# A decoder step on one core: stacked low-rank columns, values in token rows, and sample scores by head

## The reference, cut to what matters

```python
proj = h @ w_in                      # h = rmsnorm(x)
cb, cc, ch, q, k, v, g, lr = split(proj)      # 512,512,512,256,256,512,512,16 columns
log_a = log_sigmoid(lr @ gate_up + gate_b) / 16
o = gated_linear_attention(q, k, v, log_a)    # 4 heads, 64 keys, 128 values, chunks of 64
y = concat(cb * conv3(cc * ch), rmsnorm(o) * silu(g)) @ w_out
x = x + y
# cross-attention, 4 heads of 256, into 256 memory tokens; each sample has its own keys and values
q = rmsnorm(x) @ w_q
s = einsum('bthd,bmhd->bhtm', q, mk) * 256 ** -0.5
o = einsum('bhtm,bmhd->bthd', softmax(s), mv) @ w_o
x = x + o
# then a mixture of 16 experts and a last rmsnorm
```

## Time and profile before

| | us |
|---|---|
| runs shown | 1178.74, 1178.45, 1171.38 (median 1178.45) |
| the profiled execution | 1174.92 |
| its span, first to last instruction | 1173.0 |
| PE busy in it | 1090.9 (93%) |
| DVE busy | 432.6 (37%) |
| ACT busy | 361.7 (31%) |
| mean granted clock of PE | 0.958 of full speed |

### The profile page before, as it was taken

One profiled execution on the slowest core, in us unless ns is written; L12 is line 12 of the kernel. 1 busy time (PEld: TensorE's weight loads), 2 busy tenths in 40 slices (PEclk: granted clock), 3 DMA queues, 4 the chain that ended last, 5 costly groups with the idle time before them and its releaser, 6 DMA issues.

```text
span 1173.0 us, 14004 instructions
## 1 busy us (share of the span) xinstructions
PE 1090.9 (93%) x5864; PEld 860.4 (73%) x5864; DVE 432.6 (37%) x718; ACT 361.7 (31%) x563; POOL 95.6 (8%) x108
## 2 busy tenths in 40 slices
PE   7999988999999999899999989889998699999995
PEld 6778988888888879688799978658886444444442
DVE  6824421435443542633320047533127321222222
ACT  6725422211111103422122166522112111345453
POOL 1000000000000000000000000000000222344443
PEclk9998989999999998899999999989997699999998
DMA  9561011011101212432121428554225798787831
GB/s 359 165 166 36 19 54 36 19 36 37 37 19 36 78 54 60 156 109 90 56 73 37 179 94 301 218 179 162 108 91 201 287 393 338 309 335 297 329 98 59
DMA packets 85832, 167.48 MB, mean 143 GB/s; under 512 B 19050, under 2 KB 56186, under 8 KB 79364
## 3 DMA queue, kind: packets, MB, share of 16 engines
q1 hardware_dynamic: 72804, 141.14, 34.0%
q0 software_dynamic: 12960, 25.39, 6.1%
HBM read 145.03 MB, written 43.29 MB: 161 GB/s over the span
## 4 chain that ended last, share of the span: by engine, by line
PE 80%; DVE 8%; ACT 5%; DMA 4%; issue 2%; POOL 0%; POOLq 0%; SPq 0%; DVEq 0%; ACTq 0%
PE G L1354 14%; PE G L1280 12%; PE G L1282 11%; PE G L1281 11%; PE G L774 10%; PE G L796 4%; PE G L778 2%; DMA arena<-in_cache_mem_k_dram 2%; PE T L766 2%; PE T L1535 2%; PE T L1371 2%; PE G L1600 1%; PE G L801 1%; PE G L1402 1%; DMA arena<-in_w_o_dram 1%
## 5 line engine op out<-in xcount | busy, mean ns | idle before, releaser
L1280 PE MATMUL G<-act_hi,w_hi 128*128 128x344 f32 (+1 forms) x792 | 264.5, 334 | 13.7 <-DVE arena L1965 4.4
L1281 PE MATMUL G<-act_lo,w_hi 128*128 128x344 f32 (+1 forms) x792 | 257.6, 325 | 0.0
L1282 PE MATMUL G<-act_hi,w_lo 128*128 128x344 f32 (+1 forms) x792 | 257.2, 325 | 0.0
L1280 PEld LDWEIGHTS G<-act_hi,w_hi 128*128 128x128 f32 (+1 forms) x792 | 150.8, 190 | 26.8 <-issue 20.5
L1354 PE MATMUL G<-wt,act_hi 128*128 128x512 f32 x512 | 144.4, 405 | 10.4 <-DVE wt L1951 5.4
L1281 PEld LDWEIGHTS G<-act_lo,w_hi 128*128 128x128 f32 (+1 forms) x792 | 151.0, 191 | 2.6 <-issue 1.2
L1282 PEld LDWEIGHTS G<-act_hi,w_lo 128*128 128x128 f32 (+1 forms) x792 | 150.8, 190 | 1.4
L1354 PEld LDWEIGHTS G<-wt,act_hi 128*128 128x128 f32 x512 | 96.8, 192 | 34.1 <-issue 6.3
L774 PE MATMUL G<-wring,misc 128*128 128x512 f32 x256 | 114.2, 600 | 1.2 <-ACT misc L843 1.2
L666 POOL DMA_INDIRECT misc<-d_h,tidx x20 | 20.5, 1025 | 968.7 <-DVE tidx L987 911.0
L1945 DVE TENSOR_TENSOR w_lo<-arena,w_hi 128x1024 fp32r<-128x1024 f32 (+1 forms) x33 | 39.3, 1192 | 143.5 <-ACT w_hi L1652 143.5
(11 more groups left out here) (340 smaller groups left out, 1385.7 us busy)
## 6 DMA issues: line engine op xcount, KB each, us to landing
wring<-in_w_gate_dram SPq DMA_DIRECT2D x16, 1024.0 KB, 11.2
wring<-in_w_up_dram SPq DMA_DIRECT2D x16, 1024.0 KB, 13.8
wring<-in_w_down_dram SPq DMA_DIRECT2D x16, 1024.0 KB, 16.4
arena<-in_w_in_dram SPq DMA_DIRECT2D x24, 512.0 KB, 3.9
arena<-in_x_prompt_dram SPq DMA_DIRECT2D x16, 512.0 KB, 7.1
d_x<-arena SPq DMA_DIRECT2D x16, 512.0 KB
arena<-in_cache_mem_k_dram SPq DMA_DIRECT2D x8, 1024.0 KB, 7.8
arena<-in_w_k_dram SPq DMA_DIRECT2D x8, 512.0 KB, 6.3
```

Of the source, the lines that this page charges most:

```text
L1280: pe.matmul(out, a_hi, b_hi, start=first, stop=False)
L1281: pe.matmul(out, a_hi, b_lo, start=False, stop=False)
L1282: return pe.matmul(out, a_lo, b_hi, start=False, stop=last)
```

## The change

Three parts are rewritten.

First, `lr`: hi and lo parts of its 16 weight columns are placed side by side as 32 columns (`STACK`). Two matmuls per chunk, with `act_hi` and `act_lo`, take the place of three, and the 32 result rows meet `gate_up` loaded twice, so that their sum is formed in the gate's product.

Second, the values: `w_in`'s value columns are loaded as four blocks of 256 rows by 512 columns, split into the tensor `wt`, and `vtok` computes them in token rows: for nine tiles (eight of 128 tokens, one of 8 samples) 24 matmuls with the tokens as weights and 512 moving columns. Each of the first eight tiles has a PSUM bank of its own (`v_at`), and ACT copies it to `vtm`. No transposes are left. The splits of the four blocks are taken with `k0` and `k1` (the table `MORE`), ahead of `prep`. The attention's steps begin one part later (`steps = [[]]`).

Third, the memory stage: `caches` stands after the first query block. Keys are loaded in eight units, each one head of four samples (`load_keys`, 1 MB in pieces of 1 KB), and queries go to DRAM and back by head (`qh`: store, wait, broadcast of 8 samples x 256). DVE takes a unit's eight multiply-reduces (`ks`) two at a time after query blocks 3, 5 and 7, and the last two after the transposes of tiles 0 and 1. In the tiles' loop the next scores stand right behind the transposes, half of the exponentials stands ahead of them, and four of `w_o`'s splits stand before and after tile 7's transposes (`FINISH`).

```diff
-    for i in range(VB):
-        add("v", i, win, c_v + i * P)
+    for i in range(KB // 2):
+        add("v", i, win, c_v, VB * P)
...
+    MORE = {at[("k", QB - 2)]: [at[("v", i)] for i in range(2)],
+            at[("k", QB - 1)]: [at[("v", i)] for i in range(2, KB // 2)] + [at[("cc", 0)]]}
...
-        if k == "v":
-            order.append(("vT", i))
-
-    steps = []
+    order += [("vtok", t) for t in range(TILES)]
+
+    steps = [[]]
...
     for i in range(KB):
         order.append(("block", at[("mq", i)]))
...
+        h, odd = divmod(i, 2)
+        if i == 0:
+            order.append(("caches", 0))
+        if odd and 1 <= h:
+            order += [("ks", u) for u in (2 * h - 2, 2 * h - 1)]
+        if not odd and h >= 1:
+            order += [("kl", u) for u in (2 * h - 2, 2 * h - 1) if u >= 2] + [("qh", h - 1)]
+    order += [("kl", 2 * MH - 2), ("sc", 0), ("qh", MH - 1), ("kl", 2 * MH - 1), ("max", 0), ("exp", (0, 0, MH)), ("sc", 1), ("rc", 0),
+              ("scl", 0), ("max", 1), ("exp", (1, 0, 2))]
+    FINISH = {NT - 2: [("smax", 0), ("split", at[("o", 0)]), ("split", at[("o", 1)])],
+              NT - 1: [("sprob", 0), ("val", 0), ("split", at[("o", 2)]), ("split", at[("o", 3)]), ("val", 1), ("vload", 0)]}
     for t in range(NT):
         pv = [("pvk", n) for n in range((t - 2) * UP // 2, (t - 1) * UP // 2)] if t >= 2 else []
...
+        order += [("tr", t)] + [("sc", t + 2)] * two + [("exp", (t + 1, 2, MH)), ("rc", t + 1), ("scl", t + 1)] * one + pv[0:1]
+        order += [("max", t + 2), ("exp", (t + 2, 0, 2))] * two + pv[1:2]
+        if t < 2:
+            order.append(("ks", 2 * MH - 2 + t))
...
+            def load_keys(u):
+
+                h, half = divmod(u, 2)
+                sp.dma_start(keys[u % 2], cache_mem_k[0, half * HB:(half + 1) * HB, :, h, :].rearrange("b (m p) d -> p b m d", p=P)).then_inc(
+                    s[f"kc_in{u % 2}"], 16)
...
+                elif what == "kl":
+                    sp.wait_ge(s["q_sc"], i - 1)
+                    load_keys(i)
+                elif what == "qh":
+                    sp.wait_ge(s["q_ev"], i + 1)
+                    if i >= 1:
+                        sp.wait_ge(s["q_io"], 32 * i)
+                    sp.dma_start(d_q[i].rearrange("(b d) -> b d", b=DB), qs[:, i * DH:(i + 1) * DH]).then_inc(s["q_io"], 16)
+                    sp.wait_ge(s["q_io"], 32 * i + 16)
+                    if i >= 2:
+                        sp.wait_ge(s["q_sc"], 2 * (i - 1))
+                    sp.dma_start(qb[i % 2], d_q[i].partition_broadcast(P)).then_inc(s["q_io"], 16)
...
+                        if kind == "lr":
+                            pe.matmul(G[grp[u]][0:STACK, c, 0:cn], w_hi[:, slot, k, 0:STACK], act_hi[:, k, c0:c0 + cn],
+                                      start=(k == 0), stop=False)
+                            ins = pe.matmul(G[grp[u]][0:STACK, c, 0:cn], w_hi[:, slot, k, 0:STACK], act_lo[:, k, c0:c0 + cn],
+                                            start=False, stop=(k == KB - 1))
+                            continue
...
+                    for k in range(KB):
+                        p, half = divmod(k, 2)
+                        if i == 0 and half == 0:
+                            pe.wait_ge(s["split_done"], at[("v", p)] + 1)
+                        ins = mm3(v_at[i][0:r], act_hi[:, k, c0:c0 + r], act_lo[:, k, c0:c0 + r],
+                                  v_half(p, 0)[:, half, :], v_half(p, 1)[:, half, :], k == 0, k == KB - 1)
+                    ins.then_inc(s["v_mm"], 1)
...
+                    dve.wait_ge(s[f"kc_in{i % 2}"], 16 * (h + 1))
+                    dve.wait_ge(s["q_io"], 32 * (h + 1))
```

More of the change, by code:

```diff
@@ L141, in build @@
     order += [("vev", 0), ("memout", 0), ("st", 0)]
-    for n in range(2 * KB, at[("cc", 0)]):
+    for n in range(2 * KB, at[("v", 0)]):
         order.append(("block", n))
@@ L183, in build @@
     order.insert(order.index(("norm", TILES + 1)), ("split", at[("mq", 0)]))
+    PAIRS, UP = NT // 2, KB // 2
+    HB = DB // 2
     for i in range(KB):
         order.append(("block", at[("mq", i)]))
[L187 to L194, removed]
@@ L200, in build @@
[L200 to L202 removed]
+        one, two = t + 1 < NT, t + 2 < NT
+        order += [("tr", t)] + [("sc", t + 2)] * two + [("exp", (t + 1, 2, MH)), ("rc", t + 1), ("scl", t + 1)] * one + pv[0:1]
+        order += [("max", t + 2), ("exp", (t + 2, 0, 2))] * two + pv[1:2]
+        if t < 2:
+            order.append(("ks", 2 * MH - 2 + t))
+        if t == 1:
+            order.append(("kload", 0))
@@ L1140, in _ @@
             for what, i in order:
+                if what == "block" and i in MORE:
+                    for m in MORE[i]:
+                        if v_rows[m]:
+                            load_block(nb)
+                            nb += 1
                 if what in ("block", "begin") or (what == "split" and by_rows[i]):
@@ L1404, in router, with queries @@
                 ins.then_inc(s["r_mm"], 1)
+            def queries(h):
+                wait_free(pe, at[("mq", 2 * h + 1)])
+                if 1 <= h < MH - 1:
+                    pe.wait_ge(s["q_ev"], h)
+                for k in range(2):
+                    ins = pe.transpose(query_at(h)[:, k * P:(k + 1) * P], feat[:, 2 * h + k, SEQ:COLS], ident[:, :])
+                ins.then_inc(s["own_tr"], 1)
             pe.wait_ge(s["ident_rdy"], 1)
@@ L1563, in _ @@
                               stop=True).then_inc(s["gs_ms"], 1)
+                elif what == "qh" and i < MH - 1:
+                    queries(i)
                 elif what == "sc":
@@ L1787, in _ @@
                             split_hi(i + 2)
-                    elif what != "end" and i + 1 < NBLK and not by_rows[i + 1]:
+                    elif what != "end" and i + 1 < NBLK and not by_rows[i + 1] and not v_rows[i + 1]:
                         split_hi(i + 1)
+                    for m in MORE.get(i, []) if what == "block" else []:
+                        split_hi(m)
                     while behind:
@@ L2053, in _ @@
                             split_lo(i + 2)
-                    elif what != "end" and i + 1 < NBLK and not by_rows[i + 1]:
+                    elif what != "end" and i + 1 < NBLK and not by_rows[i + 1] and not v_rows[i + 1]:
                         split_lo(i + 1)
+                    for m in MORE.get(i, []) if what == "block" else []:
+                        split_lo(m)
                     while behind:
```

176 lines of the change are left out of this document (94 added, 82 removed).

## The result

The changed kernel takes 1160.63 us (median) beside 1178.6 for the kernel before in the same session: ratio 0.9862, 95% interval 0.983 to 0.9893. The forecast was 1145.0 with a range of 1136 to 1156. So the direction was right and nearly half of the gain is missing: 29.8 were announced; the ratio is worth 16.3, and the profiled execution took 1160.94, which is 14.0 less than the 1174.92 of before, with a span of 1159.0, also 14.0 less.

A forecast was written before the change was run, and what follows sets the result against it. TensorE, holding 80% of the chain that ended last, was taken as the bound. Gains of 3.7 (low-rank block), 13.1 (values) and 13.0 (memory stage), together 29.8, took 1174.9 to 1145 us; range 1136 to 1156.

The forecast's parts named there:

- The step that failed: Value stage: starting the attention steps one part of a block later was priced at nothing, three spare parts staying free.
- lr: Low-rank block ahead of the gate: 48 matmuls for 72, 3.7 us off TensorE's line, bounds 0 and 3.7.
- waited away at the gate: Rival: the low-rank block's saving is lost in waiting before the gate, giving 1149; chance 0.05.
- Values: Value stage: 216 matmuls at 0.233, 50.3 us, replace 63.4 of blocks, transposes and waits; 13.1 gained.
- the late casts: Rival in the value stage: four casts come late and tile 0 waits 3 to 4, giving 1148; chance 0.04.
- The rival of 512-column matmuls at 0.131: Value stage: matmuls with 512 columns run faster by 0.1 each, 216 of them, giving 1123; chance 0.01.
- Queries and keys: Query blocks: score units and query round trips fit beside TensorE's work; slack 5.3 at head 2's predecessors, nothing lost.
- Nothing is lost and nothing is to spare: Head 2: units 4 and 5 end at 680.9, just before the prompt's first maximum at 680.97.
- The rival of 9.2: Query broadcast takes 9.2 instead of 4.8, so the first maximum slips by 4.4: 1149 to 1154; chance 0.15.
- The attention loop: Memory stage: tiles 2 to 5 at 7.8 each, tile 6 at 5.0, idle 5.6 near the end; 13.0 gained.
- the rival that the tail's wait only changes its name: Memory stage's end: 12.0 of idle stays, ScalarE's casts replacing the w_o loads, giving 1151; chance 0.10.
- The lower bound of this term, 5.4: Memory stage: smallest gain allowed for the tile loop and its tail; 13.0 counted, bounds 5.4 and 20.

The follow-up runs named there:

- e1: The changed kernel without the empty first step, so attention steps stand at the conv parts as before: 1149.68 us, ratio 0.9771 to the kernel before.
- e3: The changed kernel with only VectorE's order edited: ch taps behind the next attention step, normalizations behind the conv evacuation they preceded: 1145.99 us, ratio 0.9743.
- e4: The changed kernel with four empty steps ahead of the attention steps, all of the spare ones: 1162.36 us, ratio 0.9884 to the kernel before.
- e2: The kernel before with only one empty step added ahead of the attention steps: 1183.36 us, ratio 1.0057.
- the long trip: The changed kernel with each head's store of the queries, and the wait for it, made four times instead of once: 1162.93 us, ratio 0.9873.
- e8: The kernel before with only VectorE's order edited (taps behind the next attention step, normalizations behind conv evacuations): 1178.41 us, ratio 1.0021.

## Why the prediction was wrong

The step that failed is one sentence: "Moving the attention steps back by one part of a block costs nothing, since three of the four spare parts stay free." It cost 12.5 in the profile. The parts were counted and not what DVE has to do in them: without a delay two of the three places of collision (33 and 35) are spare parts where no step stands, and the delay puts steps on all three places (6, 8 and 32). The rows for it were at hand: in the kernel before, PE waits 2.36 on the one collision that it has, with a reciprocal of 3.35 in front of the evacuation.

```profile
330.87 3.35 DVE L2132 RECIPROCAL arena<-arena 128x512 f32<-128x512 f32 x1 [10.94 <-ACT arena L1852]
...
334.86 1.23 DVE L1965 TENSOR_TENSOR arena<-G,arena 128x1032 f32<-128x1032 f32 x1
```

```profile
336.23 0.40 PE L1280 MATMUL G<-act_hi,w_hi 128*128 128x344 f32 x1 [2.36 <-DVE arena L1965]
```

That the delay costs it, through the order of DVE's queue, is shown by e1, e3 and e4, and by e2 in the kernel before. The size is less sure than the cause: 12.5 in the profiles, 10.7 in e1 by the ratios, 7.5 in e2, and the clock alone moves the stretch by 3 from one execution to another. With the failed step mended on DVE alone (e3) the time is 1145.99, beside the 1145.0 of the sum. That is closer than the sum deserves, and luck: the delay moves the collision of the kernel before away (its wait of 2.36 at the third ch block is 0.61 in the change), the edit takes the three new ones, and two places at half clock fewer than before remain. So the conv stretch is 4.8 shorter than before (209.93 and 205.13), which covers the 3.3 that are missing elsewhere in the change.

The other terms, point by point.
- lr: 11.20 became 7.51, 3.69 for 3.7. It was not waited away at the gate; that rival falls.
- Values: 50.0 for 50.3, no wait inside, so the late casts didn't come; first conv part 16.5 earlier for 16.8. The rival of 512-column matmuls at 0.131 falls. The Trainium skill, "TensorE: Matmul & The Clock Gate", section "Back-to-back issue gap", gives about 131 ns for a sustained matmul of N=512; this run shows 231.5, so the measurement decides.
- Queries and keys: every time within 0.6. "Nothing is lost and nothing is to spare" at head 2 holds to about 0.6; the long trip shows it. The broadcast took 4.6 to 5.1 from its issue to the first score, for 4.8 (issued at 619.07, 641.81 and 664.57, scores at 624.16, 646.66 and 669.61; in the long trip 619.41 and 664.92, scores at 624.31 and 669.54). The rival of 9.2 falls.
- The attention loop: 11.4 for 13.0. Tiles 3 to 6 stand 7.8 apart, as forecast, and the rival that the tail's wait only changes its name, a gain of 6.6, falls. Idle behind tile 7's transposes was 3.3 (2.59, 0.40, 0.33) for 5.6. Two things were mis-sized. One is the clock: I allowed one stretch at half clock, 1.2, and there were two, the scores behind tile 2 (5.0 for 3.46, a loss of 1.6) and the value products at 743.95, which took 4.86 where others take 3.62. The other is tile 6: 6.7 for the 5.0 of the sum, with waits of 0.86 and 0.85. Tile 2, earlier than forecast, and the shorter idle time at the end gave part of both back. The lower bound of this term, 5.4, doesn't follow from what the prediction shows: 14.2 less 6.4 and 1.2 is 6.6, the 1151 of its rival.
- Of the remaining 1.4, 0.6 is the samples' transposes that moved into the query blocks; the other 0.8 (0.2 there and 0.6 behind the loop) I can't put on a wait.

The rivals were all about the new parts; none was about work that the change only shifts. The prediction's own text gave the cover as a count of slots and named no queue.

## What to carry to other kernels

When a hand-written order is shifted, even by an empty slot, write out what every engine finds in its queue at each slot, before and after: a step that is free on one engine moves its followers on the others. Put what another engine waits for ahead of work that has time, and look what the moved work meets next, since e8 only renamed its wait. A stall of 2 to 3 us on a full TensorE must be priced with the clock behind it: here 4.8 more of idle came with 7.8 of lower clock, most of it behind the three waits.

## What the runs showed of the hardware

The clock lost behind a stall can be dearer than the stall (after the wait of 2.50, about 5), and isn't the same each time. The change and the kernel with the long trip have the same waits and the same idle time of 12.7 in the conv stretch, and take 222.47 at a granted clock of 0.93 and 219.37 at 0.95: 3.1 us between two executions of the same order there. After the wait of 2.50 PE ran 12 us at 0.57 although it had no idle time at all in them; that wait stands directly in front of a step `go`, so these 12 us have both in them. The Trainium skill, "TensorE: Matmul & The Clock Gate", section "A second HAM failure mode: psum-queue depth-cycling", tells of short idle times between groups of matmuls, with a clock that falls and rises again and again. The places behind the three waits agree with it; those behind a step `go` don't, since PE had no idle time ahead of them (from 252 to 260 it was busy 8.00 of 8.00, at 0.79). Of the eight steps `go`, three had half clock behind them in the kernel before, four in the change (five with the one behind the wait of 2.50) and two in e3; what decides it no run here shows. Whether a single wait of a given length brings a stretch at half clock I can't say either: the wait of 1.42 to 1.47 at the fourth ch block had none behind it in any of the nine kernels that have it, those of 2.3 to 3.4 nearly always had one (in the long trip one of 2.4 had none).
